# Split weights and inputs for gated-linear units 1 to 7, and v normalised by ACT, in a one-core encoder step

## The chip, the cores and the metric

The kernel runs on one core of a Trainium2 chip. The metric is the device time of one execution in microseconds (us). The engines of the core are named as in the profile: PE (matrix products), ACT (activations and copies), DVE (vector work), POOL (GpSimd), SP (issues most of the DMAs).

## What is computed

One step of a one-layer encoder on 512 prompt tokens and 32 sample tokens (T = 544 in all, D = 1024 features). The part that the change touches:

```python
z = h @ w_in + b_in                       # h: normalised, modulated input, 544 x 1024
a = glu(z[..., 0:2048])                   # first half * sigmoid(second half)
a = silu(layer_norm(depthwise_causal_conv(concat(history, a), conv_w, conv_b), ln_g, ln_b))
y_a = a @ w_a
u, v = gelu(z[..., 2048:3072]), gelu(z[..., 3072:4096])
v = layer_norm(v, v_ln_g, v_ln_b)         # v of the 32 sample rows is an output
y_b = (u * (tril(w_s) mixed over 128 positions of v + b_s)) @ w_b
merged = sigmoid(gates_a) * y_a + sigmoid(gates_b) * y_b
x = x + g1 * (merged @ w_o)
```

After it comes a mixture of 32 experts (top group, then top 2 of 8 in it) and a final norm. All inputs and outputs are float32.

## The kernel before, in words

Features lie on the partitions and tokens along the row, so that a product of 128 output features is `PS[128, 544]`, made in two halves of 272 columns. The mixer runs in stages, and each engine's order is written out by hand with semaphores.

- **GLU units 0 to 7** (`product`, L552). Unit n makes features 128n to 128n+127 of both halves of `a`, so two products, in plain float32 from `WP` (weights) and `hT` (input). ACT drains each unit (L989, L990, the last one the sigmoid; semaphore `act_drained`). SP may load unit n+2 into unit n's buffer when unit n is done (`w_used`).
- **v** (L656): nine groups in float32, drained by ACT through a gelu (L1020) into `v`, tokens on the partitions.
- **u units 0 to 3** (`product_split`, L619). Here a float32 factor is split in a high part (rounded to fp32r by an ACT copy: `wH` L1002, `gH` L998) and the rest (`wL`, `gL`, a DVE or POOL subtraction), and the product is the sum of three fp32r products, high by high, high by low and low by high. DVE makes the `wL` of the u units (`low_u`, L1277), each of them two instructions, one for each product; ACT makes the `wH` (`high_of`).
- **Gate units** 0 to 15 (`gate(j)`), two to each load, also in three products. POOL makes their `wL` (`low_gate`, L1699), two instructions for each pair of gates.
- **The mixing** (`mix(h)`, L683) needs `v` normalised (`v_norm`); a mean over features by PE (`over_features`, L690) waits for the sum of the convolved tiles (`conv_sum`).

DVE is the engine with the long job here: the depthwise convolution, 31 taps for each of 8 tiles of 574 columns, a pair of tiles at a time (i = 0, 2, 4, 6), two `scalar_tensor_tensor` for each tap (L1295). A pair begins when ACT has drained both of its units (`act_drained`). `low_u(0)` stands after pair 4, `low_u(1)` to `low_u(3)` after taps 9, 17 and 25 of pair 6. Then `add_tiles` sums the eight tiles (L1308, signals `conv_sum`), and then DVE takes the statistics of v (L1320), scales and shifts it (L1330 to L1332, `v_norm`) and subtracts the mean from the tiles (L1336, `centred`).

POOL's queue after the constants is `low_gate` 0 to 2, a store of the sample rows of v, `low_gate` 3 to 5, eight squares (L1713) and `low_gate` 6 to 15.

## Time and profile before

| | us |
|---|---|
| median of 3 runs (lowest, highest) | 937.46 (935.69, 938.75) |
| the profiled execution, its own time | 940.93 |
| its span, first to last instruction | 939.1 |
| PE busy | 837.4 (89%) |
| DVE busy | 504.8 (54%) |
| ACT busy | 191.3 (20%) |
| POOL busy | 156.5 (17%) |

The profiled execution is 3.5 us above the median. Its mean granted clock of PE is 0.949 of full speed. The page of the profile has one line for each group of instructions; a start is counted from the first instruction of the span. An instruction's duration may overlap the next one's on the same engine, so that the interval from start to start is the cost in a stream.

### The profile page before, as it was taken

The numbers are of one execution on the slowest core, as the hardware profiler recorded it, in microseconds if no ns is written. First come the engines' busy times: TensorE is split into PE (matmuls) and PEld (weight loads), VectorE is DVE, ScalarE is ACT, GpSimd is POOL, SyncE is SP. The second block draws the span as 40 slices with busy tenths as digits, with TensorE's granted clock in tenths as the row PEclk, the third lists the DMA queues.
The fourth block names the chain that finished last, engine by engine and source line by source line (L and its number), as shares of the span: only waits on it lengthen the run. The fifth ranks groups of instructions, "written<-read, shape, count | busy, mean of one in ns | idle before, by whom it ended". The sixth has DMA issues, their size and how long they took to land. (4 is left out here: it accounts for less than half of the span.)

```text
span 939.1 us, 12130 instructions
## 1 busy us (share of the span) xinstructions
PE 837.4 (89%) x4994; PEld 610.1 (65%) x4994; DVE 504.8 (54%) x754; ACT 191.3 (20%) x286; POOL 156.5 (17%) x152
## 2 busy tenths in 40 slices
PE   2899999999999999899999999628999988797776
PEld 1588887345999999798777544625666655454432
DVE  1427999999999735703755344661333331312236
ACT  4211121101225213821200022101111111111003
POOL 1000000000033345342322000011222221211110
PEclk9899999999999999999999999558999989989899
DMA  9932232211223313459899580614999999999926
GB/s 320 304 95 79 56 89 90 90 45 45 79 62 96 96 46 90 123 193 309 300 329 331 205 350 24 277 61 171 414 406 416 414 417 378 391 388 411 381 76 249
DMA packets 112600, 204.16 MB, mean 217 GB/s; under 512 B 9484, under 2 KB 68212, under 8 KB 104350
## 3 DMA queue, kind: packets, MB, share of 16 engines
q1 hardware_dynamic: 94192, 159.36, 47.8%
q10 hardware_dynamic: 12830, 34.93, 9.6%
q0 software_dynamic: 5520, 9.06, 2.6%
q8 instruction: 41, 0.67, 0.3%
q14 instruction: 17, 0.14, 0.0%
HBM read 199.49 MB, written 14.84 MB: 228 GB/s over the span
## 5 line engine op out<-in xcount | busy, mean ns | idle before, releaser
L862 PE MATMUL PS<-arena 128*64 128x256 f32 (+1 forms) x1056 | 148.6, 411 | 31.6 <-issue 26.5
L1295 DVE SCALAR_TENSOR_TENSOR arena<-arena,VT 128x574 f32<-128x574 f32 x240 | 175.2, 817 | 0.0
L862 PEld LDWEIGHTS PS<-arena 128*64 128x64 f32 (+1 forms) x1056 | 107.3, 157 | 68.1 <-issue 41.9
L1699 POOL TENSOR_TENSOR wL<-arena,wH 128x1024 fp32r<-128x1024 f32 x32 | 82.6, 2604 | 373.1 <-ACT wH L1002 373.1
L552 PE MATMUL PS<-arena 128*128 128x272 f32 x512 | 120.6, 399 | 1.6 <-DVE arena L1257 1.6
L552 PEld LDWEIGHTS PS<-arena 128*128 128x128 f32 x512 | 99.2, 194 | 22.6 <-issue 1.6
L1595 DVE TENSOR_TENSOR arena<-PS,arena 128x256 f32<-128x256 f32 x19 | 8.1, 425 | 141.5 <-ACT arena L1129 141.5
L619 PE MATMUL PS<-gH,wH 128*128 128x272 f32 x384 | 80.2, 290 | 1.9 <-DVE wL L1277 1.2
L619 PE MATMUL PS<-gH,wL 128*128 128x272 f32 x384 | 79.8, 289 | 0.0
L619 PE MATMUL PS<-gL,wH 128*128 128x272 f32 x384 | 79.7, 289 | 0.0
L882 PE MATMUL PS<-arena 128*64 128x512 f32 (+1 forms) x264 | 69.1, 597 | 1.4 <-DVE arena L1599 1.4
L1002 ACT ACTIVATE wH<-arena 128x1024 fp32r<-128x1024 f32 x40 | 40.2, 1052 | 122.8 <-DMA arena<-w_in 52.2
L1743 POOL DMA_INDIRECT pairs<-arena,sidx x19 | 30.4, 1600 | 193.4 <-DVE arena L1611 193.4
L619 PEld LDWEIGHTS PS<-gH,wH 128*128 128x128 f32 x384 | 59.9, 188 | 3.3 <-ACT arena L1020 1.5
L619 PEld LDWEIGHTS PS<-gH,wL 128*128 128x128 f32 x384 | 60.5, 188 | 0.0
L619 PEld LDWEIGHTS PS<-gL,wH 128*128 128x128 f32 x384 | 60.1, 188 | 0.0
L619 PE MATMUL PS<-yH,wH 128*128 128x272 f32 x256 | 54.7, 295 | 4.5 <-issue 4.5
L756 PE MATMUL PS<-arena 128*128 128x512 f32 x128 | 55.7, 593 | 0.7 <-DMA arena<-w_o 0.7
L656 PE MATMUL PS<-arena 128*128 128x512 f32 x128 | 56.2, 592 | 0.0
L619 PE MATMUL PS<-yH,wL 128*128 128x272 f32 x256 | 53.5, 290 | 0.0
L1129 ACT ACTIVATE arena<-PS 128x256 f32<-128x256 f32 x19 | 7.3, 384 | 210.2 <-PE PS L862 210.2
L619 PEld LDWEIGHTS PS<-yH,wH 128*128 128x128 f32 x256 | 40.4, 191 | 14.8 <-issue 11.4
(276 smaller groups left out, 978.4 us busy)
## 6 DMA issues: line engine op xcount, KB each, us to landing
arena<-w_gate SPq DMA_DIRECT2D x32, 1024.0 KB, 11.2
arena<-w_up SPq DMA_DIRECT2D x32, 1024.0 KB, 16.7
arena<-w_down ACTq DMA_DIRECT2D x28, 1024.0 KB, 15.2
arena<-w_ada SPq DMA_DIRECT2D x12, 2048.0 KB, 10.4
arena<-w_in SPq DMA_DIRECT2D x40, 512.0 KB, 5.2
arena<-w_ada_f SPq DMA_DIRECT2D x4, 2048.0 KB, 8.9
arena<-x_prompt SPq DMA_DIRECT2D x8, 512.0 KB, 8.2
arena<-w_in SPq DMA_DIRECT2D x4, 1024.0 KB, 6.4
```

Of the source, the lines that this page charges most:

```text
L552: last = pe.matmul(PS[:, bank + h, 0:H], tile_w[:, k, :], act[:, k, h * H:(h + 1) * H], start=(k == 0), stop=(k == KT - 1))
L619: last = pe.matmul(PS[:, bank + h, 0:H], w[:, k, :], part[:, k, h * H:(h + 1) * H], start=(k == 0 and n == 0), stop=(k == KT - 1 and n == 2))
L656: last = pe.matmul(PS[:, bank, :], hT[:, k, t * P:(t + 1) * P], W[hf][:, k, :], start=False, stop=(k == KT - 1))
L756: last = pe.matmul(PS[:, (2 * t + hf) % 8, :], mT[:, k, t * P:(t + 1) * P], W[hf][:, k, :], start=(k == 0), stop=(k == KT - 1))
L862: last = pe.matmul(PS[h * rows:(h + 1) * rows, 2, n * DE:(n + 1) * DE], hG[:, b, k * SLOTS + h * rows:k * SLOTS + (h + 1) * rows], buf[r / ...
L882: last = pe.matmul(PS[h * rows:(h + 1) * rows, 4 + 2 * b + hf, :], heT[:, k, h * rows:(h + 1) * rows], WD[r // 2][r % 2][:, k, hf * 512:(h ...
L1002: act.activation(wH2[n % 2][:, m], WP[n % 2][:, m], ACT.Copy).then_inc(gw_high, 1)
L1129: act.activation(sil, PS[:, 2, 0:DE], ACT.Silu).then_inc(sil_ready, 1)
L1295: dve.scalar_tensor_tensor(out=total, in0=src, scalar=tap, in1=total, op0=ALU.mult, op1=ALU.add).then_inc(conv_step, 1)
L1595: dve.tensor_tensor(he, PS[:, 2, DE:2 * DE], sil, ALU.mult).then_inc(he_ready, 1)
L1699: pool.tensor_tensor(wL2[q % 2][:, m], WP[q % 2][:, m], wH2[q % 2][:, m], ALU.subtract).then_inc(gw_split, 1)
L1743: pool.indirect_dma_start(out=pairs, out_offset=bass.IndirectOffsetOnAxis(ap=sidx[b][:, 0:1], axis=0), in_=Y[:, b, :], in_offset=None, bou ...
```

## The change

The rest of this section names lines of the kernel before. Unit 0 stays as it was. Units 1 to 7 of the GLU are made by `product_split`: ACT copies their high parts (`high_a`), DVE subtracts (`low_a`), all of `gH` is copied before unit 0's drain and all of `gL` subtracted before the first pair of the convolution. The `low_a` of units 3 to 7 stand inside pair 0 of the convolution, the `low_u` inside pairs 4 and 6, after other taps than before. Two new products on PE sum the rows of the mixing matrix (`rowsum_ps`); DVE folds `v_ln_b` times these sums into `bsb`, and multiplies by `v_ln_g` where it drains the mixing.

v is no longer normalised by DVE. The gelus of ACT write their sums, DVE makes the mean after tap 28 of pair 4, ACT squares and sums (five instructions) and takes the root, DVE makes scale and offset after tap 4 of pair 6, and ACT applies them (five instructions) after it has drained the first u unit. POOL then makes the 32 output rows of v with weight and bias (two instructions) ahead of `low_gate(0)`. `over_features` of the mean stands after `gate(3)`, before it stood after `gate(2)`. Of `b_in`, `v_ln_g` and `v_ln_b` only 1, 32 and 32 rows are loaded instead of 128 each, and 16 rows more go through the start's transposes.

```diff
+            for q in range(2):
+                last = pe.matmul(PS[:, 4 + q, :], meanm[:, :], wsT[:, 4 * q:4 * q + 4, :].rearrange("p h t -> p (h t)"), start=True, stop=True)
+            last.then_inc(rowsum_ps, 1)
+
+            def product_split(bank, w_high, w_low, act_high, act_low, split=None, split_of=None):
...
+                if n == 1:
+                    pe.wait_ge(rowsum_used, 1)
                 for m in range(2):
-                    last = product(4 * b + 2 * m, WP[b][:, m], hT, first=(n == 0))
+                    if n == 0:
+                        last = product(2 * m, WP[0][:, m], hT, first=True)
+                        continue
+                    pe.wait_ge(aw_split, 2 * n + m - 1)
+                    last = product_split(4 * b + 2 * m, wH2[b][:, m], wL2[b][:, m], gH, gL, 0 if (n, m) == (1, 0) else None, g_split)
...
             histories(FULL - HIST)
             gate(2)
+            gate(3)
             pe.wait_ge(conv_sum, 1)
             pe.wait_ge(hist_copied, 2)
             over_features(6, rstdc)
-            gate(3)
             gate(4)
             gate(5)
...
+            def high_a(n):
+                full(act, U_A + n)
+                for m in range(2):
+                    act.activation(wH2[n % 2][:, m], WP[n % 2][:, m], ACT.Copy).then_inc(aw_high, 1)
+
+            high_a(1)
+            act.wait_ge(h_odd, KT)
+            act.wait_ge(h_even, KT)
+            for j in range(KT):
+                act.activation(gH[:, j, :], hT[:, j, :], ACT.Copy).then_inc(g_high, 1)
             for n in range(KT):
                 b = 4 * (n % 2)
...
-                if n == 2:
-                    act.wait_ge(h_even, KT)
-                    act.wait_ge(h_odd, KT)
-                    act.wait_ge(bias_split, 3)
-                if n in (2, 3, 4, 5):
-                    for j in (2 * n - 4, 2 * n - 3):
-                        act.activation(gH[:, j, :], hT[:, j, :], ACT.Copy).then_inc(g_high, 1)
+                if n + 2 < KT:
+                    high_a(n + 2)
...
+                    total = {} if t == 4 else {"accum_out": vsum[:, t, hf:hf + 1]}
+                    act.activation(v[0:WIDTH[t], t, hf * 512:(hf + 1) * 512], src, ACT.Gelu_apprx_tanh, **total).then_inc(v_gelu, 1)
+                if g == 2:
+                    act.wait_ge(v_gelu, 4)
+                    act.activation(mg[0:NSAMPLE, :], v[0:NSAMPLE, 4, :], ACT.Copy, accum_out=vsum[0:NSAMPLE, 4, 0:1]).then_inc(v_sample, 1)
                 if g == 6:
                     high_of(U_U)
             high_of(U_U + 1)
+            act.wait_ge(v_mean, 1)
+            for t in range(TT):
+                w = WIDTH[t]
+                if t:
+                    act.wait_ge(v_sq, t)
+                act.activation(mg[0:w, :], v[0:w, t, :], ACT.Square, bias=mv[0:w, 0, t:t + 1], accum_out=vvar[0:w, t:t + 1]).then_inc(v_sq, 1)
+            act.wait_ge(v_sq, TT)
+            act.activation(vsd[:, 0:TT], vvar[:, 0:TT], ACT.Sqrt, bias=eps[:, :], scale=1.0 / D).then_inc(v_sd, 1)
...
+                if n == 0:
+                    act.wait_ge(v_scale, 1)
+                    for t in range(TT):
+                        vt = v[0:WIDTH[t], t, :]
+                        act.activation(vt, vt, ACT.Identity, scale=vsd[0:WIDTH[t], t:t + 1], bias=mv[0:WIDTH[t], 1, t:t + 1]).then_inc(v_norm, 1)
...
+            def low_a(n):
+                for m in range(2):
+                    dve.wait_ge(aw_high, 2 * n + m - 1)
+                    dve.tensor_tensor(wL2[n % 2][:, m], WP[n % 2][:, m], wH2[n % 2][:, m], ALU.subtract).then_inc(aw_split, 1)
+
+            then(dve.tensor_scalar(VT[:, COL_VB:COL_VB + KT], VT[:, COL_VB:COL_VB + KT], float(D), None, ALU.mult))
+            low_a(1)
+            for j in range(KT):
+                dve.wait_ge(g_high, j + 1)
+                dve.tensor_tensor(gL[:, j, :], hT[:, j, :], gH[:, j, :], ALU.subtract).then_inc(g_split, 1)
+
             dve.wait_ge(bc_in, 64)
+            dve.wait_ge(rowsum_ps, 1)
+            for h in range(KT):
+                soon(dve.scalar_tensor_tensor(out=bsb[:, h, :], in0=PS[:, 4 + h // 4, (h % 4) * P:(h % 4 + 1) * P], scalar=VT[:, COL_VB + h:COL_VB + h + 1],
+                                              in1=bsb[:, h, :], op0=ALU.mult, op1=ALU.add))
             then(dve.memset(b3, 0.0))
-            rest, piece = bvb[0:1, :], mod1[0:1, 0:D]
+            dve.sem_inc(rowsum_used)
+            rest, piece = bvb[0:1, :], mg[0:1, :]
...
+            low_a(2)
+            LOW_A = {(0, 3): 3, (0, 9): 4, (0, 16): 5, (0, 23): 6, (0, 29): 7}
+            LOW_U = {(4, 14): 0, (4, 27): 1, (6, 3): 2, (6, 10): 3}
...
-                    if i == 6 and k in (9, 17, 25):
-                        low_u((k - 1) // 8)
-                if i == 2:
-                    dve.wait_ge(g_high, KT)
-                    for j in range(KT):
-                        dve.tensor_tensor(gL[:, j, :], hT[:, j, :], gH[:, j, :], ALU.subtract).then_inc(g_split, 1)
-                if i == 4:
-                    low_u(0)
+                    if (i, k) in LOW_A:
+                        low_a(LOW_A[i, k])
+                    if (i, k) in LOW_U:
+                        low_u(LOW_U[i, k])
+                    if (i, k) == (4, 28):
+                        dve.wait_ge(v_gelu, 10)
+                        dve.wait_ge(v_sample, 1)
+                        then(dve.tensor_tensor(mv[:, 1, :], vsum[:, :, 0], vsum[:, :, 1], ALU.add))
+                        dve.tensor_scalar(mv[:, 0, :], mv[:, 1, :], -1.0 / D, None, ALU.mult).then_inc(v_mean, 1)
+                    if (i, k) == (6, 4):
+                        dve.wait_ge(v_sd, 1)
+                        then(dve.reciprocal(vsd[:, 0:TT], vsd[:, 0:TT]))
+                        dve.tensor_tensor(mv[:, 1, :], mv[:, 0, :], vsd[:, 0:TT], ALU.mult).then_inc(v_scale, 1)
...
-            dve.wait_ge(bc_in, 64)
-            for t in range(TT):
-                w = WIDTH[t]
-                dve.wait_ge(v_gelu, 7 + t if t < 4 else 4)
-                for hf in range(2):
-                    then(dve.bn_stats(bn[0:w, hf, :], v[0:w, t, hf * 512:(hf + 1) * 512]))
-                last = dve.bn_aggr(mv[0:w, t, :], bn[0:w, :, :].rearrange("p a b -> p (a b)"))
-                if t < TT - 1:
-                    then(last)
-            last.then_inc(v_var, 1)
-            dve.wait_ge(v_sd, 1)
-            then(dve.reciprocal(vsd[:, 0:TT], vsd[:, 0:TT]))
-            for t in range(TT):
-                w = WIDTH[t]
-                vt = v[0:w, t, :]
-                then(dve.tensor_scalar(vt, vt, mv[0:w, t, 0:1], vsd[0:w, t:t + 1], ALU.subtract, ALU.mult))
-                then(dve.tensor_tensor(vt, vt, vgb[0:w, :], ALU.mult))
-                dve.tensor_tensor(vt, vt, vbb[0:w, :], ALU.add).then_inc(v_norm, 1)
-
...
-                                  PS[:, 4 + 2 * b, :].rearrange("p (c t) -> p c t", t=P),
-                                  bsb[:, h:h + 1, :].to_broadcast([P, 4, P]), ALU.add).then_inc(mix_added, 1)
-                dve.tensor_tensor(tmp[:, b, NPROMPT:T], PS[:, 5 + 2 * b, 0:NSAMPLE], bsb[:, h, 0:NSAMPLE], ALU.add).then_inc(dve_drained, 1)
+                gain = VT[:, COL_VG + h:COL_VG + h + 1]
+                dve.scalar_tensor_tensor(out=tmp[:, b, 0:NPROMPT].rearrange("p (c t) -> p c t", t=P),
+                                         in0=PS[:, 4 + 2 * b, :].rearrange("p (c t) -> p c t", t=P), scalar=gain,
+                                         in1=bsb[:, h:h + 1, :].to_broadcast([P, 4, P]), op0=ALU.mult, op1=ALU.add).then_inc(mix_added, 1)
+                dve.scalar_tensor_tensor(out=tmp[:, b, NPROMPT:T], in0=PS[:, 5 + 2 * b, 0:NSAMPLE], scalar=gain,
+                                         in1=bsb[:, h, 0:NSAMPLE], op0=ALU.mult, op1=ALU.add).then_inc(dve_drained, 1)
...
+            pool.wait_ge(bc_in, 64)
+            pool.wait_ge(v_norm, TT)
+            rows = vgb[0:NSAMPLE, :]
+            pool.tensor_tensor(rows, v[0:NSAMPLE, 4, :], rows, ALU.mult).then_inc(v_gained, 1)
+            pool.wait_ge(v_gained, 1)
+            pool.tensor_tensor(rows, rows, vbb[0:NSAMPLE, :], ALU.add).then_inc(v_shifted, 1)
             low_gate(0)
-            low_gate(1)
-            low_gate(2)
-            pool.wait_ge(v_norm, TT)
-            pool.dma_start(v_out, v[0:NSAMPLE, 4, :]).then_inc(v_stored, 16)
-            low_gate(3)
-            low_gate(4)
-            low_gate(5)
+            pool.wait_ge(v_shifted, 1)
+            pool.dma_start(v_out, rows).then_inc(v_stored, 16)
+            for q in range(1, 6):
+                low_gate(q)
             pool.wait_ge(mix_ps, KT)
```

The first place is POOL's queue between the constants and the experts, in the kernel before. Line 1699 is `low_gate`, two rows for each of its calls, and line 1713 the squares.

```order
L1692 AFFINE_SELECT arena<-arena 128x128 x8
L1699 TENSOR_TENSOR wL<-arena,wH 128x1024 x6
L1705 DMA v_rows<-arena 32x1024
L1699 TENSOR_TENSOR wL<-arena,wH 128x1024 x6
L1713 TENSOR_TENSOR arena<-arena 128x574 x8
```

The same place in the changed kernel, where line 1742 is `low_gate` and lines 1747 and 1749 make the output rows of v:

```order
L1735 AFFINE_SELECT arena<-arena 128x128 x8
L1747 TENSOR_TENSOR arena<-arena 32x1024
L1749 TENSOR_TENSOR arena<-arena 32x1024
L1742 TENSOR_TENSOR wL<-arena,wH 128x1024 x2
L1752 DMA v_rows<-arena 32x1024
L1742 TENSOR_TENSOR wL<-arena,wH 128x1024 x10
L1758 TENSOR_TENSOR arena<-arena 128x574 x8
```

Two instructions that wait for the normalised v now stand ahead of the first `low_gate`.

The second place is DVE's last pair of the convolution before. Line 1295 is a tap of one tile, line 1277 `low_u`, line 1308 the sum of the tiles.

```order
L1292 TENSOR_SCALAR arena<-arena,VT 128x574 x2
L1295 SCALAR_TENSOR_TENSOR arena<-arena,VT 128x574 x18
L1277 TENSOR_TENSOR wL<-arena,wH 128x1024 x2
L1295 SCALAR_TENSOR_TENSOR arena<-arena,VT 128x574 x16
L1277 TENSOR_TENSOR wL<-arena,wH 128x1024 x2
L1295 SCALAR_TENSOR_TENSOR arena<-arena,VT 128x574 x16
L1277 TENSOR_TENSOR wL<-arena,wH 128x1024 x2
L1295 SCALAR_TENSOR_TENSOR arena<-arena,VT 128x574 x10
L1308 TENSOR_TENSOR rstdc<-arena 128x574
```

The same pair in the changed kernel (line 1348 is a tap, 1327 `low_u`, 1360 and 1361 the scale and offset of v, 1366 the sum):

```order
L1345 TENSOR_SCALAR arena<-arena,VT 128x574 x2
L1348 SCALAR_TENSOR_TENSOR arena<-arena,VT 128x574 x6
L1327 TENSOR_TENSOR wL<-arena,wH 128x1024 x2
L1348 SCALAR_TENSOR_TENSOR arena<-arena,VT 128x574 x2
L1360 RECIPROCAL vsd<-vsd 128x5
L1361 TENSOR_TENSOR mv<-mv,vsd 128x5
L1348 SCALAR_TENSOR_TENSOR arena<-arena,VT 128x574 x12
L1327 TENSOR_TENSOR wL<-arena,wH 128x1024 x2
L1348 SCALAR_TENSOR_TENSOR arena<-arena,VT 128x574 x40
L1366 TENSOR_TENSOR rstdc<-arena 128x574
```

The last `low_u` moved from ten taps ahead of the end of the pair to forty ahead of it.

## Rows read from the trace of the kernel before

**Rows 1.** Busy time of each engine in stretches of the span, with clock.

```profile
core 0: us, PE busy (x) PEld busy (x) DVE busy (x) ACT busy (x) POOL busy (x), PEclk, DMA share, GB/s
42.00:60.00 18.00, 17.21 (x62) 13.85 (x63) 8.96 (x16) 4.04 (x8) 0.00 (x0) 0.81 0.39 127
...
280.00:350.00 70.00, 69.67 (x543) 67.85 (x542) 50.34 (x69) 23.72 (x28) 27.12 (x13) 1.00 0.30 81
...
392.00:400.00 8.00, 3.50 (x18) 3.39 (x17) 3.58 (x6) 7.80 (x13) 0.00 (x0) 0.81 0.87 270
...
650.00:939.00 289.00, 249.69 (x1470) 152.60 (x1466) 89.45 (x110) 44.08 (x69) 53.66 (x69) 0.94 0.91 363
```

**Rows 2.** Timeline of PE: start, duration, instruction, count [idle before it].

```profile
42.79 120.57 PE L552 MATMUL PS<-arena 128*128 128x272 f32 x512 [1.57 <-DVE arena L1257]
...
229.90 0.52 PE L619 MATMUL PS<-gH,wH 128*128 128x272 f32 x2 [0.69 <-ACT arena L1020]
...
299.67 1.13 PE L690 MATMUL PS<-rstdc,meanm 128*128 128x287 f32 x4
...
318.78 1.05 PE L683 MATMUL PS<-wsT,arena 128*128 128x128 f32 x8
```

**Rows 3.** Timeline of ACT: sums with a read-out, table, drains of units.

```profile
12.87 1.06 ACT L952 ACTIVATE tmp<-arena 128x1024 f32<-128x1024 f32 x1
...
14.11 1.05 ACT L952 ACTIVATE tmp<-arena 32x1024 f32<-32x1024 f32 x1
...
15.28 1.28 ACT L954 ACT_TABLE_LOAD   x1
...
75.40 1.02 ACT L989 ACTIVATE arena<-PS,VT 128x272 f32<-128x272 f32 x3 [11.54 <-PE PS L552]
...
90.07 1.02 ACT L989 ACTIVATE arena<-PS,VT 128x272 f32<-128x272 f32 x3 [13.04 <-PE PS L552]
...
242.29 1.32 ACT L1033 ACTIVATE arena<-PS,VT 128x544 f32<-128x544 f32 x2 [4.27 <-PE PS L619]
248.16 2.01 ACT L1002 ACTIVATE wH<-arena 128x1024 fp32r<-128x1024 f32 x2 [4.55 <-DMA arena<-w_in]
254.40 1.32 ACT L1033 ACTIVATE arena<-PS,VT 128x544 f32<-128x544 f32 x2 [4.22 <-PE PS L619]
...
280.00 1.32 ACT L1033 ACTIVATE arena<-PS,VT 128x544 f32<-128x544 f32 x2 [5.68 <-PE PS L619]
```

**Rows 4.** Timeline of DVE: pair 0, the split of the inputs, a `low_u`.

```profile
77.06 1.50 DVE L1284 TENSOR_TENSOR arena<-arena 128x512 f32<-128x512 f32 x4 [19.70 <-ACT arena L990]
...
79.58 43.72 DVE L1295 SCALAR_TENSOR_TENSOR arena<-arena,VT 128x574 f32<-128x574 f32 x60
...
169.35 5.17 DVE L1301 TENSOR_TENSOR gL<-arena,gH 128x544 fp32r<-128x544 f32 x8
...
238.45 2.36 DVE L1277 TENSOR_TENSOR wL<-arena,wH 128x1024 fp32r<-128x1024 f32 x2
```

**Rows 5.** Timelines of POOL and DVE at the end of the convolution.

```profile
273.45 4.71 POOL L1699 TENSOR_TENSOR wL<-arena,wH 128x1024 fp32r<-128x1024 f32 x1 [248.12 <-ACT wH L1002]
...
272.88 3.02 DVE L1295 SCALAR_TENSOR_TENSOR arena<-arena,VT 128x574 f32<-128x574 f32 x4
275.94 2.84 DVE L1308 TENSOR_TENSOR rstdc<-arena 128x574 f32<-128x574 f32 x1
```

**Rows 6.** Timelines of POOL and DVE where both subtract and multiply.

```profile
385.79 2.97 POOL L1699 TENSOR_TENSOR wL<-arena,wH 128x1024 fp32r<-128x1024 f32 x1 [6.63 <-ACT wH L1002]
...
385.76 0.76 DVE L1365 TENSOR_TENSOR arena<-arena,rstdc 128x574 f32<-128x574 f32 x1
...
386.43 2.94 DVE L1365 TENSOR_TENSOR arena<-arena,rstdc 128x574 f32<-128x574 f32 x1
```

**Rows 7.** A POOL copy during a DVE instruction of the convolution's kind.

```profile
650.27 0.97 POOL L1739 COPY sidx<-pairI 128x1 uint32<-128x1 uint32 x1
...
649.91 1.29 DVE L1603 SCALAR_TENSOR_TENSOR tmp<-arena,wsel,tmp 128x1024 f32<-128x1024 f32 x1 [0.64 <-ACT tmp L1135]
```

46 lines of the change are left out of this document (23 added, 23 removed).

## The prediction, made before the changed kernel ran

> **What bounds the kernel now.** I read the table of stretches first, to see which engine is full and at what clock. From 280 to 350 us PE is busy for 69.67 of 70 us at clock 1.00, while DVE is busy for 50.34 and POOL for 27.12 [rows 1]. The late stretch, 650 to 939, is one of weight loads, with the DMA engines 0.91 busy; each load there waits for a buffer that the stage before has freed, so a delay or a gain of the mixer passes on whole. Then I read PE's timeline. The GLU stage is one block of 120.57 us from 42.79, the first u unit begins at 229.90, the mean over features stands at 299.67 and the first mixing at 318.78 [rows 2]. So in this kernel PE sets the end of the mixer. The third view, the timelines of DVE and POOL, asks whether PE stays the bound once it is faster. DVE runs its convolution without a break from 77.06 [rows 4] to the first sum at 275.94 [rows 5], 198.9 us. PE asks POOL for the first `low_gate` only when the u units are through, at 280.00 [rows 3]. Those two jobs hardly meet in the kernel before.
>
> **PE's own gain.** Two drains of float32 units lie 90.07 - 75.40 = 14.67 us apart, two of units in three products 254.40 - 242.29 = 12.11 us [rows 3]. Seven units save 7 x 2.56 = 17.9 us. Unit 0 before ended at 75.40 - 14.67 = 60.7. Two row sums of 512 columns now stand ahead of it, four records of float32. The rate of the float32 units (64 records of 272 columns in 14.67 us, so 0.43 us for 512) makes them 1.7 us at the full clock and 3.5 at half. That stretch has clock 0.81 over 18 us [rows 1], so it lost 3.4 us at half speed; PE now works without a pause from before unit 0, and its clock may rise sooner (unit 0 ends at 59.7) or as late as before (61.6). Unit 1 also needs both splits, the folding into `bsb` and a memset on DVE, some 11 us of ACT's and DVE's time after ACT's loads are issued, which is the same range. I take 60.5. Unit 7 then ends at 60.5 + 84.8 = 145.3. The v stage and its waits took 229.90 - 163.36 = 66.5, and the read-outs of the gelus add 0.2 at the last one, as two squares with a read-out are 14.11 - 12.87 = 1.24 us apart though one lasts 1.06 [rows 3]. The first u unit can start at 212.0, 17.9 us earlier than before.
>
> Does DVE keep up in the GLU stage? The drained unit's load, ACT copy and DVE subtraction need 248.16 - 242.29 = 5.9, then 1.0, then 1.2 us, in all 8.1 of the 12.1 that PE gives [rows 3, 4]. The `low_a` lie 6 or 7 taps apart, and a tap of two tiles costs 43.72 / 30 = 1.457, so one round is at most 10.2 + 2.4 = 12.6 us; starting with 2.3 us of slack they never make PE wait. I cost this at nothing.
>
> **DVE's job.** It begins 1.7 us after unit 1, as before (77.06 against 75.40), at 60.5 + 12.1 + 1.7 = 74.3. Against the 198.9 us: the split of the inputs goes out of it, -5.2; five `low_a` come in at 2.36, +11.8 [rows 4]; four instructions of five columns, +0.8. The u splits only move. The chain for v adds a wait. DVE makes the mean at 74.3 + (46.1 + 11.8) + 46.1 + 2.6 + 40.8 + 4.7 + 0.5 = 226.9 (pairs 0 and 2, the start of pair 4, 28 taps, two `low_u`); behind it ACT needs 5 x 1.24 for the squares, 1.28 + 0.3 for table and root, 1.28 for the next table, 1.32 for the drain of the first u unit and 1.0 for the next copy, and it is at 238.3. PE, ready for its third u unit at 236.2, starts it at 239.6, and DVE itself waits 1.3 us at that `low_u`. Without POOL the convolution thus ends at 74.3 + 198.9 - 5.2 + 11.8 + 0.8 + 1.3 = 281.9, 6 us later than before, although PE comes 14 us sooner. The statistics and scaling of v, which lay behind the sum of tiles, are gone from DVE, but PE was full from 280 to 350 [rows 1] and hardly waited for them, so that this is worth nothing by itself.
>
> **POOL beside the convolution.** This decides. PE now wants `low_gate(0)` at about 265, with 20 us of taps still to come; before it wanted it at 280, after them. The one row that shows a POOL subtraction issued inside the taps took 4.71 us. Four taps ran from 272.88 to 275.9, at their usual distance; three of them began after POOL's issue at 273.45, and then DVE's first sum, at 275.94, took 2.84 in place of the 0.76 of this size [rows 6], until POOL was done at 278.16 [rows 5]. A subtraction alone is 2.35 us (in [rows 6] POOL has the port from 386.41, when DVE's first instruction ends, to 388.76), so POOL began at 275.8, with the end of the last tap. A short POOL copy issued inside an instruction of the same kind ended with it, at 651.2 [rows 7]. So a tap keeps POOL out, and in a stream of taps POOL didn't get in at three boundaries out of three. In the likeliest case POOL's `low_gate(0)` therefore waits for the end of the convolution. The two output rows of v get in around the last `low_u`, where DVE's instructions are plain ones of two inputs, and cost 2 x 2.35: the convolution ends at 286.6. POOL's first subtraction is done at 289.0, and PE's gates begin there and not at 279.9, +9.1. PE has then stood for over 20 us. After a pause of 4.5 us the stretch from 392 to 400 had clock 0.81, which is 1.5 us lost; the start lost 3.4 [rows 1]. I take 2.4 between these. Behind that PE is the bound again: `conv_sum` comes at 286.6 + 7 sums of 0.79 + 4 POOL instructions = 301.5, and PE reaches the mean at 315. The sum is +9.1 + 2.4 = +11.5 us.
>
> The profiled execution has 939.1 of span and 940.93 of time, so it would become 952.4; on the median of the runs, 937.46, it is 949.0.
>
> The smaller edits cost nothing: the multiplication in the mixing's drain has one input in PSUM and hides in DVE's waits for the mixings; the two start loads and the smaller broadcasts lie beside PE's wait for weights; the later `over_features` only takes up a wait for `conv_sum`.
>
> **Rivals.** (a) POOL gets in at each boundary. Where DVE multiplies plainly, POOL, issued at 385.79, took 2.97, so it got in at the first boundary, and DVE's second instruction took 2.94 in place of 0.76 [rows 6]. That speaks for it; the taps of [rows 5] against. Then eight POOL instructions (two rows, six of `low_gate`) each push the taps by 2.2: the convolution ends at 281.9 + 17.6 = 299.5, the sum of tiles (5.5) with two more POOL instructions at 309.4. PE, early at its gates, waits for `conv_sum` and comes to the first mixing 1.1 + 12.1 later, at 322.6 against 318.78, +3.8, and 2.4 of clock make +6.2: 943.7. The Trainium skill, SBUF — State Buffer, section "SBUF: two separate sides", says that the shared port pair is an exclusive lock, that a DVE instruction with two SBUF inputs and a GpSimd one that reads SBUF compete for it, and that whichever starts first has it for the whole instruction. By that page POOL, which asks before the next tap, is this rival; the trace agrees on the lock [rows 6, 7] and not on who gets it [rows 5].
>
> (b) The other side: POOL doesn't disturb and is not disturbed, the long row in [rows 5] being only the first instruction of its kind on POOL. Then the `low_gate` come when called, the sum is done at 287.4, the u units end at 265, four gates and two histories at 291.3, and the first mixing begins at 304.5, -14.3: 923.2. It decides by the number of POOL instructions that fall ahead of the sum of tiles: with seven the sum comes at 302.8 and the first mixing at 316.0, and with 2.4 of clock the time is that of before; with none it is this. For it: PE's gain is real. Against it: [rows 6, 7].
>
> (c) Between: POOL gets in for the first `low_gate` but rarely after, and PE and DVE wait less for each other. Six POOL instructions ahead of the sum of tiles put it at 300.6 and the first mixing at 313.8, with the clock 934.9; nine put them at 307.2 and 320.4, with the clock 941.5.
>
> **How the numbers follow.** Chances: 0.50 for the forecast, 0.24 for (a), 0.13 for (b), 0.13 for (c), of which 0.08 lies within 0.3% (2.8 us, about what a measurement can tell from no change). So faster 0.13, same 0.08, slower 0.79. The low end of the range takes in (a), with its clock term at nothing too (941.3), and the upper part of (c), and leaves out (b) and the lower part of (c): 939. The high end is the forecast with the later unit 0 (+1.1), the larger clock term (+1.0) and POOL's rows behind the convolution too (+1.6), with a run's spread above it: 954.
>
> **What would show it.** In the changed profile: two GLU drains 12.1 us apart; the first u unit near 212; the last tap between 285 and 289; POOL's first subtraction of 128 x 1024 with a duration of over 20 us, and an idle time of PE of about 22 us that ends on it. If POOL's subtractions there last 2.4 to 3.2 us and taps of 3 us lie between the others, it is (a), and PE waits for `conv_sum`. If the taps keep their 0.73 and POOL its 2.35 at the same time, it is (b), and I am wrong about the port.

## The result, and the profile after

The changed kernel takes 942.31 us (median of 6 runs, 941.58 to 943.55) against 938.11 us for the kernel before on the same chip (6 runs, 935.69 to 943.84). The ratio is 1.0043, 95% interval 1.0024 to 1.0063: slower by 4 us, where 11.5 us slower was forecast. The profiled execution took 941.58 us, its span is 939.8 us and its mean granted clock 0.937. It lies 0.7 below its median, and that of before 2.8 above, so the two spans differ by 0.7 us only; I come back to this at the end of the section.

The stretches that answer to [rows 1], and two more, 270 to 290 and 290 to 310, which in the kernel before had PE busy throughout at clock 1.00:

```profile
42.00:60.00 18.00, 18.00 (x81) 14.63 (x80) 13.54 (x28) 10.95 (x20) 0.00 (x0) 0.95 0.32 58
270.00:290.00 20.00, 7.18 (x59) 6.78 (x56) 19.96 (x27) 7.58 (x9) 19.91 (x1) 0.74 0.24 65
290.00:310.00 20.00, 18.98 (x127) 18.77 (x128) 15.48 (x12) 1.43 (x2) 9.51 (x4) 0.84 0.16 45
392.00:400.00 8.00, 2.81 (x12) 2.85 (x13) 3.08 (x4) 7.94 (x12) 0.46 (x1) 0.72 0.92 282
```

PE has a new hole: from 270 to 290 it is busy for 7.18 us, while DVE is full and POOL shows one instruction that fills the stretch. Behind the hole the clock is 0.84 over 20 us; it is 0.50 from 291.02, where PE starts again, to 296.54, so 2.8 us of PE's work are lost there. PE's timeline, which answers to [rows 2]:

```profile
39.94 3.18 PE L616 MATMUL PS<-wsT,meanm 128*128 128x512 f32 x4
42.91 15.35 PE L556 MATMUL PS<-arena 128*128 128x272 f32 x64
58.08 0.48 PE L626 MATMUL PS<-gH,wH 128*128 128x272 f32 x2
...
209.69 0.52 PE L626 MATMUL PS<-gH,wH 128*128 128x272 f32 x2 [0.78 <-ACT arena L1040]
...
237.39 0.48 PE L626 MATMUL PS<-gH,wH 128*128 128x272 f32 x2 [3.24 <-DVE wL L1327]
...
291.02 0.82 PE L626 MATMUL PS<-gH,wH 128*128 128x272 f32 x2 [13.84 <-POOL wL L1742]
...
318.71 1.05 PE L695 MATMUL PS<-wsT,arena 128*128 128x128 f32 x8
```

The first u unit begins 20.2 us earlier than before. Two waits follow, and the first mixing begins at 318.71, where it began before (318.78). The whole gain of the three products is gone by then. The wait of 13.84 us stands ahead of gate 2: gates 0 and 1 and both history steps, 14.0 us of PE's work, were made before it, from 263.2 to 277.2. The drains of units on ACT, which answer to [rows 3], are 12.10 and 12.11 us apart, and the last u unit is drained at 263.38, 16.6 earlier than before:

```profile
70.46 1.02 ACT L1013 ACTIVATE arena<-PS,VT 128x272 f32<-128x272 f32 x3 [4.36 <-PE PS L626]
...
82.56 1.02 ACT L1013 ACTIVATE arena<-PS,VT 128x272 f32<-128x272 f32 x3 [3.65 <-PE PS L626]
...
94.67 1.02 ACT L1013 ACTIVATE arena<-PS,VT 128x272 f32<-128x272 f32 x3 [4.37 <-PE PS L626]
...
263.38 1.32 ACT L1064 ACTIVATE arena<-PS,VT 128x544 f32<-128x544 f32 x2 [3.80 <-PE PS L626]
```

POOL's timeline, which answers to [rows 5]:

```profile
246.10 7.26 POOL L1747 TENSOR_TENSOR arena<-arena 32x1024 f32<-32x1024 f32 x1 [220.37 <-ACT arena L1072]
253.44 2.78 POOL L1749 TENSOR_TENSOR arena<-arena 32x1024 f32<-32x1024 f32 x1
258.71 5.44 POOL L1742 TENSOR_TENSOR wL<-arena,wH 128x1024 fp32r<-128x1024 f32 x2 [2.49 <-ACT wH L1021]
264.10 0.75 POOL L1752 DMA_DIRECT2D v_rows<-arena  x1
270.09 29.42 POOL L1742 TENSOR_TENSOR wL<-arena,wH 128x1024 fp32r<-128x1024 f32 x4 [5.24 <-ACT wH L1021]
```

and DVE's, which answers to [rows 4, 5]:

```profile
72.11 1.50 DVE L1337 TENSOR_TENSOR arena<-arena 128x512 f32<-128x512 f32 x4 [4.57 <-ACT arena L1014]
...
248.77 2.35 DVE L1327 TENSOR_TENSOR wL<-arena,wH 128x1024 fp32r<-128x1024 f32 x2
251.04 37.72 DVE L1348 SCALAR_TENSOR_TENSOR arena<-arena,VT 128x574 f32<-128x574 f32 x40
288.80 2.78 DVE L1366 TENSOR_TENSOR rstdc<-arena 128x574 f32<-128x574 f32 x1
291.61 10.89 DVE L1366 TENSOR_TENSOR rstdc<-rstdc,arena 128x574 f32<-128x574 f32 x6
```

Here lies the answer. POOL was neither shut out throughout nor let in throughout. I call a tap pushed when it lasts about 2.95 us in place of 0.80, because POOL's instruction goes first. The first row of v waited for the end of the `low_u` at 251; the second row and both subtractions of `low_gate(0)` got in among the taps (5.44 us for two). The first subtraction of `low_gate(1)`, asked for at 270.09, was shut out until the last tap: of the row of four in 29.42 us it takes 20.88, and the others, which push DVE's first sums, 2.88 to 2.90 each. On DVE's side forty taps take 37.72 us. Where POOL does nothing among them they take 29.17 (below), so the four pushes (two rows of v, two subtractions) cost 2.14 us each.

**Where the 4 us are.** At the first mixing the two kernels are level. The drain of the first branch unit comes 1.3 us later, since PE's wait ahead of it is 5.55 instead of 4.50 us and the stretch from 392 to 400 has clock 0.72 instead of 0.81. In the router the distance is 1.05 us, by the same DVE instruction in both traces, first that of before, then that of after:

```profile
621.58 0.83 DVE L1554 TENSOR_TENSOR arena<-arena,iota 128x640 f32<-128x640 f32 x1
```

```profile
622.63 0.83 DVE L1595 TENSOR_TENSOR arena<-arena,iota 128x640 f32<-128x640 f32 x1
```

From there to the end it is 317.5 us before and 317.2 after. So the traces show 1.1 us of loss; the other 3 us of the medians lie in no stretch that these two executions show, and their cause stays open. On another chip one run of the changed kernel took 939.6 us against a median of 938.59 before.

### The profile page after: what moved, and what is told of

Read it like the earlier page. It is cut to its first block and busy times, and to the rows that moved or that the text cites. A ratio compares the mean times of both kernels' runs of the same rounds, so it can differ in the third digit from the quotient of the medians.

```text
span 939.8 us, 12626 instructions
## 1 busy us (share of the span) xinstructions
PE 824.3 (88%) x5222; PEld 611.1 (65%) x5222; DVE 511.5 (54%) x750; ACT 218.8 (23%) x324; POOL 184.2 (20%) x156
## 5 line engine op out<-in xcount | busy, mean ns | idle before, releaser
L1348 DVE SCALAR_TENSOR_TENSOR arena<-arena,VT 128x574 f32<-128x574 f32 x240 | 184.3, 841 | 0.0
L873 PEld LDWEIGHTS PS<-arena 128*64 128x64 f32 (+1 forms) x1056 | 105.5, 157 | 67.6 <-issue 42.0
L626 PE MATMUL PS<-gH,wH 128*128 128x272 f32 x608 | 127.8, 292 | 17.9 <-POOL wL L1742 13.8
L626 PE MATMUL PS<-gH,wL 128*128 128x272 f32 x608 | 128.0, 292 | 0.0
L626 PE MATMUL PS<-gL,wH 128*128 128x272 f32 x608 | 127.9, 292 | 0.0
L1742 POOL TENSOR_TENSOR wL<-arena,wH 128x1024 fp32r<-128x1024 f32 x32 | 100.1, 3150 | 136.1 <-ACT wH L1021 136.1
L626 PEld LDWEIGHTS PS<-gH,wH 128*128 128x128 f32 x608 | 96.2, 191 | 19.8 <-POOL wL L1742 14.1
L626 PEld LDWEIGHTS PS<-gH,wL 128*128 128x128 f32 x608 | 97.5, 192 | 0.0
L626 PEld LDWEIGHTS PS<-gL,wH 128*128 128x128 f32 x608 | 96.7, 191 | 0.0
L1747 POOL TENSOR_TENSOR arena<-arena 32x1024 f32<-32x1024 f32 x1 | 7.3, 7262 | 220.4 <-ACT arena L1072 220.4
L893 PEld LDWEIGHTS PS<-arena 128*64 128x64 f32 (+1 forms) x264 | 22.4, 145 | 34.1 <-issue 32.5
```

Of the source, the lines that this page charges most:

```text
L626: last = pe.matmul(PS[:, bank + h, 0:H], w[:, k, :], part[:, k, h * H:(h + 1) * H], start=(k == 0 and n == 0), stop=(k == KT - 1 and n == 2))
L873: last = pe.matmul(PS[h * rows:(h + 1) * rows, 2, n * DE:(n + 1) * DE], hG[:, b, k * SLOTS + h * rows:k * SLOTS + (h + 1) * rows], buf[r / ...
L893: last = pe.matmul(PS[h * rows:(h + 1) * rows, 4 + 2 * b + hf, :], heT[:, k, h * rows:(h + 1) * rows], WD[r // 2][r % 2][:, k, hf * 512:(h ...
L1348: dve.scalar_tensor_tensor(out=total, in0=src, scalar=tap, in1=total, op0=ALU.mult, op1=ALU.add).then_inc(conv_step, 1)
L1742: pool.tensor_tensor(wL2[q % 2][:, m], WP[q % 2][:, m], wH2[q % 2][:, m], ALU.subtract).then_inc(gw_split, 1)
```

## The experiments

The theory at the start: POOL waits for DVE at the port that the two share, and what is shut out, and when, sets the end. Its rivals: PE or ACT's order sets it, or the shutting out is chance. All times of before are from the same chip as the run beside them.

**The same kernel again.** No edit.

> The changed kernel once more, for its trace alone. If the way POOL is shut out of the taps of the convolution is fixed by the order of the instructions, the same rows come again: the first output row of v (L1747) lasts 7 us, the first subtraction of low_gate(1) about 20 us, and PE waits 13 to 14 us for it. If it is chance, other POOL instructions are the long ones, and the wait is anywhere between 0 and 20 us.

One run: 939.6 us (before 938.59). Everything from the first u unit on came some 1.6 us later, yet POOL's pattern is the same: 7.28, 2.78, then `low_gate(0)` in 2.40 and 2.90, then 20.36 us for the first subtraction of `low_gate(1)`; PE waits 13.9 us. The same instructions are shut out in both executions, so the order of work decides, not chance.

**Gates on DVE.** Everything stays but who makes the `wL` of gates 0 to 5, and that the rows of v stand behind `low_gate(4)`.

```diff
+            LOW_G = {(6, 17): 0, (6, 24): 1}
...
+                    if (i, k) in LOW_G:
+                        low_g(LOW_G[i, k])
...
             add_tiles(cv)
+            low_g(2)
...
-            low_gate(0)
-            for q in range(1, 6):
-                low_gate(q)
+            for q in range(3, 5):
+                low_gate(q)
```

> low_gate 0, 1 and 2 go from POOL to DVE (after taps 17 and 24 of the last pair, and after the sum of the tiles), and the two output rows of v go behind low_gate(4) on POOL. Theory 1 (the shared port: POOL's instructions are shut out of the taps, and push them when they get in): no POOL instruction meets a tap any more; DVE pays 4 x 1.15 inside the taps in place of 5 x 2.2, the last tap ends near 282, the sum near 288, PE reaches the mean over features near 290 and the first mixing near 303, so 12 to 15 us faster than the changed kernel: 927 to 931. Theory 2 (DVE's own work is too long, whoever subtracts): the sum of tiles comes at 295 or later and the gain is under 6 us: 936 or more.

925.18 us (924.12 to 925.72), ratio to before 0.9856 (0.9837 to 0.9875): 13.4 us faster than before. By the two ratios to before it is some 17 us faster than the change; against the one run of the change on this chip, 939.6, it is 14.4. PE's and DVE's timelines:

```profile
289.98 1.24 PE L702 MATMUL PS<-rstdc,meanm 128*128 128x287 f32 x4 [1.13 <-DVE rstdc L1374]
...
303.31 1.05 PE L695 MATMUL PS<-wsT,arena 128*128 128x128 f32 x8
```

```profile
263.12 10.26 DVE L1354 SCALAR_TENSOR_TENSOR arena<-arena,VT 128x574 f32<-128x574 f32 x14
...
284.41 0.76 DVE L1374 TENSOR_TENSOR rstdc<-arena 128x574 f32<-128x574 f32 x1
```

The two `low_g` beside these taps cost DVE 2.35 us each, 4.7 in all, where four pushes cost 8.6, the hole in PE is gone, and the first mixing begins 15.5 us earlier than before. So PE's gain was real, and POOL beside the taps took it. (This kernel changes two things; the rows of v moved by themselves are tried below, and that makes it slower.) The time is some 2 us better than the best I expected.

**ACT's order too.** The kernel above, with `low_g` after taps 14 and 22, and ACT's squares behind the drain of the first u unit.

```diff
-            act.wait_ge(v_mean, 1)
...
+                if n == 0:
+                    act.wait_ge(v_mean, 1)
...
                 high_of(U_U + n + 2)
```

> The changed kernel with low_gate 0 to 2 on DVE (0 and 1 after taps 14 and 22 of pair 6, 2 behind the sum of tiles), and with ACT's squares of v behind the drain of the first u unit instead of ahead of it, so that the copy for the third u unit isn't late. Theory 1 (POOL shut out cost the time, and the 3.2 us wait of PE for low_u is ACT's order): in the run with the gates on DVE alone PE still waited 3.2 us for DVE's wL and had a piece at half clock behind it; this wait falls under 1 us, and the time is 921 to 924 us, ratio to before 0.982 to 0.985. Theory 2 (DVE's sum of tiles is the bound then, and PE only waits there for what it gained): the wait before the mean over features grows from 1.1 us by what PE gained, first mixing at 302 to 303.5 us, time 924 to 926.

925.53 us (922.56 to 928.57), ratio 0.9866 (0.9842 to 0.989). PE's waits in the u units fell to 0.99 and 1.21 us and it reached the mean over features earlier, but the sum was not there:

```profile
288.60 1.24 PE L702 MATMUL PS<-rstdc,meanm 128*128 128x287 f32 x4 [1.96 <-DVE rstdc L1375]
...
303.46 1.05 PE L695 MATMUL PS<-wsT,arena 128*128 128x128 f32 x8
```

The mean starts 1.4 us earlier than in the kernel above, since the sum is done earlier (288.54 against 289.92), and the clock takes that back: it is 0.91 from 290 to 310, and 1.00 in the kernel above. Theory 2 has the first mixing and the time right and theory 1 has not: PE's 3.2 us wait for `low_u` was worth nothing here, in part because DVE's sum is the bound and in part by the clock.

**Pauses.** The changed kernel; from tap 12 of pair 6, each second tap waits until the one before it has ended.

```diff
-                            dve.wait_ge(conv_step, i * TAPS + (2 * (k - 1) + b + 1))
+                            dve.wait_ge(conv_step, i * TAPS + (2 * k if i == 6 and k > 11 and b == 0 else 2 * (k - 1) + b + 1))
```

> From tap 12 of the last pair each pair of taps waits until the tap just before it has ended, so that DVE stands still for about 0.1 us every 1.5 us; nothing else is changed. Theory 1 (POOL gets in wherever DVE pauses): the first subtraction of low_gate(1) lasts under 5 us in place of 20.9, PE waits not for POOL but for the sum of the tiles, which comes 2 us later than in the changed kernel for the pauses and no earlier, since the POOL instructions now push taps in place of sums: the mean over features near 304, the time 939 to 943. If PE's wait for POOL were all that costs, the time would be near 930. Theory 3 (POOL is kept out by something else than the seamless stream of taps): the 20 us row stays, and the time is 943 to 946.

945.76 us (942.45 to 947.58), ratio 1.0073 (1.0048 to 1.0098). POOL, DVE and PE:

```profile
271.17 5.83 POOL L1742 TENSOR_TENSOR wL<-arena,wH 128x1024 fp32r<-128x1024 f32 x2 [6.38 <-ACT wH L1021]
283.61 5.44 POOL L1742 TENSOR_TENSOR wL<-arena,wH 128x1024 fp32r<-128x1024 f32 x2 [6.61 <-ACT wH L1021]
296.74 5.15 POOL L1742 TENSOR_TENSOR wL<-arena,wH 128x1024 fp32r<-128x1024 f32 x2 [7.69 <-ACT wH L1021]
```

```profile
251.61 52.47 DVE L1348 SCALAR_TENSOR_TENSOR arena<-arena,VT 128x574 f32<-128x574 f32 x40
```

```profile
309.68 2.28 PE L702 MATMUL PS<-rstdc,meanm 128*128 128x287 f32 x4 [19.85 <-DVE rstdc L1366]
```

A pause of 0.1 us is enough: from tap 12 on every POOL instruction gets in, the 20.88 us are gone, and PE has its gates in time. But ten POOL instructions now fall among the taps (the second row of v and four pairs of subtractions, the first row behind the `low_u`), forty taps take 52.47 us, and PE waits 19.85 us for the sum instead. The sum is done at 309.62 and the first mixing begins at 325.01, before at 318.78. Letting POOL in costs about as much as shutting out `low_gate(0)` does (325.71 and a ratio of 1.0072, under "The rows of v last"). The time lies 3 us above what I expected and within the 943 to 946 of theory 3, but the trace, with the 20 us row gone, speaks for theory 1; the later convolution also caught `low_gate(3)`, two more pushes that I had not counted.

**The GLU half alone.** Units 1 to 7 in three products, the `low_u` and the mean over features placed as in the change; v is normalised by DVE as before and POOL makes no rows.

```diff
-                    last = product(4 * b + 2 * m, WP[b][:, m], hT, first=(n == 0))
+                    pe.wait_ge(aw_split, 2 * n + m - 1)
+                    last = product_split(4 * b + 2 * m, wH2[b][:, m], wL2[b][:, m], gH, gL, 0 if (n, m) == (1, 0) else None, g_split)
```

> The GLU half of the change alone: units 1 to 7 in three products, with the low_u and the mean over features placed as in the changed kernel; v is normalised by DVE behind the sum of tiles as before. Theory 1: the taps end at 282 to 288, the sum by 297, and 28 to 32 us of statistics and scaling follow, so that v is ready near 325 to 330 in place of 315, and PE waits there: 945 to 952. If DVE's queue did not matter, this half alone would give PE's 17 us: near 922.

950.45 us (947.66 to 952.17), ratio 1.0129 (1.0103 to 1.0155), +11.9 us.

```profile
255.49 32.92 POOL L1719 TENSOR_TENSOR wL<-arena,wH 128x1024 fp32r<-128x1024 f32 x4 [230.44 <-ACT wH L1013]
```

```profile
248.47 29.17 DVE L1319 SCALAR_TENSOR_TENSOR arena<-arena,VT 128x574 f32<-128x574 f32 x40
```

```profile
279.98 0.79 PE L620 MATMUL PS<-gH,wH 128*128 128x272 f32 x2 [20.09 <-POOL wL L1719]
...
321.59 1.05 PE L688 MATMUL PS<-wsT,arena 128*128 128x128 f32 x8
...
326.31 1.96 PE L688 MATMUL PS<-wsT,arena 128*128 128x128 f32 x8 [3.34 <-DVE arena L1356]
```

This is the forecast's mechanism: `low_gate(0)` is shut out from 255.5 to the last tap, 24.35 us for one subtraction. PE stands 20.09 us, and another 3.34 for the centred tiles, since DVE's work on v is on the path here. The time is in the range that I expected, but mostly for another reason: I had expected the wait for v alone and not the 20.09 us for POOL.

**The rows of v last.** The changed kernel with POOL's two rows behind `low_gate(4)`.

```diff
+            for q in range(0, 5):
+                low_gate(q)
             pool.wait_ge(bc_in, 64)
...
-            low_gate(0)
```

> The changed kernel with POOL's two output rows of v moved behind low_gate(4); DVE, ACT and PE unchanged. Theory 1 (whether POOL gets in is decided for each instruction by how it falls among the taps, and one that is issued in the middle of a seamless stream is mostly shut out to its end, as with the GLU half alone): low_gate(0), now issued near 253 to 255 us, lasts until the last tap, over 20 us, PE waits some 18 to 20 us for POOL before gate 0, last tap near 280 us (no pushes), time 942 to 950 us. Theory 2 (POOL gets in at about every second boundary by chance of its arrival): low_gate(0) lasts 2.4 to 3.2 us, low_gate(1) may be shut out, PE's wait stays near 14 us or less, time 938 to 943 us.

946.69 us (941.33 to 947.66), ratio 1.0072 (1.0049 to 1.0095).

```profile
259.76 33.40 POOL L1742 TENSOR_TENSOR wL<-arena,wH 128x1024 fp32r<-128x1024 f32 x4 [234.00 <-ACT wH L1021]
```

```profile
284.67 0.82 PE L626 MATMUL PS<-gH,wH 128*128 128x272 f32 x2 [20.00 <-POOL wL L1742]
...
325.71 1.05 PE L695 MATMUL PS<-wsT,arena 128*128 128x128 f32 x8
```

Two short instructions taken out of the way, and `low_gate(0)` is shut out for 24.86 us where it took 2.58. The taps go through unpushed, PE waits 20.00, and the first mixing comes 6.9 us later than before and 7.0 later than in the changed kernel, of which 1.9 were there at the first u unit (211.61 against 209.69). So the rows of v were what opened the door for `low_gate(0)` in the changed kernel.

**Bursts of POOL in the kernel before.** At four places of the convolution POOL multiplies three times on scratch memory; memsets of different sizes ahead of them shift where in a tap POOL asks. (Added work; ACT waits for it, so the times, 965.40 and 965.37 us, say nothing.)

```diff
+            for at, size in zip((20, 82, 144, 194), (0, 128, 256, 512)):
+                pool.wait_ge(conv_step, at)
+                if size:
+                    one(pool.memset(tmp2[:, 1, 0:size], 0.0))
+                both()
+                both()
+                one(pool.memset(tmp2[:, 1, 0:384], 0.0))
+                both()
```

> The kernel before with four bursts of POOL work on scratch memory during the convolution (each three multiplications of 128x1024, with a memset ahead of two of them), so the time is longer and not of interest. Theory 1 (a waiting POOL instruction is let in by a gap between DVE's instructions, such as a low_a, a low_u or the end of a pair, and by a boundary between two taps only sometimes): some of the 12 multiplications last 2.3 to 3.3 us, others over 5 us, up to the next instruction of DVE that is no tap; each one that gets in makes one tap 2.9 us long. Theory 2 (a tap always loses at its end to a waiting POOL instruction): all 12 last under 3.4 us. Theory 3 (the time within a tap at which POOL's instruction is issued decides): short and long ones separate by the distance from the last tap's start.

> The same bursts behind memsets of other sizes, so that the multiplications are issued at other distances from a tap's start. Theory 3: short and long ones separate at the same distance as in the other probe. Theory 1: both kinds occur at equal distances. Theory 2: all last under 3.4 us.

Two bursts of the first of them:

```profile
91.42 36.54 POOL L1710 TENSOR_TENSOR tmp<-arena 128x1024 f32<-128x1024 f32 x2 [65.96 <-DVE arena L1296]
...
128.72 2.50 POOL L1710 TENSOR_TENSOR tmp<-arena 128x1024 f32<-128x1024 f32 x1
...
143.86 40.96 POOL L1710 TENSOR_TENSOR tmp<-arena 128x1024 f32<-128x1024 f32 x2
```

In all eight bursts the first multiplication is shut out: in pairs 0, 2 and 4 through every tap that is left of the pair, in pair 6 until the next `low_u` has ended (34.0, 38.1, 35.2 and 12.5 us; 33.8, 38.6, 34.9 and 12.8 in the other kernel), while the second and third, asked for 0.1 and at most 0.8 us behind the end of POOL's last multiplication, are done in 2.85 us at most, the third among taps as well. The point within a tap plays no part: first ones were asked for at 0.07 to 0.69 us into one. A boundary of another kind isn't safe either: the 38.1 us went past the end of the taps and all eight subtractions of 128x544 from 173.92 on. The memsets, which read nothing, last 0.15 to 0.63 us and are never held up for the length of a tap. Theories 2 and 3 fall. Theory 1, that a gap of another kind lets POOL in, is right in part only, and does not say when a boundary between taps does.

**How long the door stays open.** One tap pauses, POOL asks k taps later, and a second pause follows 8 taps behind the call; nine times in each kernel.

```diff
+                            at = i * TAPS + 2 * k + b
+                            dve.wait_ge(conv_step, at if at in PAUSES else at - 1)
...
+            for n, at in enumerate((7, 27, 47, 72, 92, 112, 137, 157, 177)):
+                pool.wait_ge(conv_step, at)
+                pool.tensor_tensor(tmp2[:, 1, 0:1024], vgb[:, 0:1024], vbb[:, 0:1024], ALU.mult).then_inc(probed, 1)
```

> The kernel before, with nine POOL multiplications of 128x1024 on scratch memory in pairs 0, 2 and 4 of the convolution. Each is asked for k taps behind a tap that had to wait until the one before it had ended (a pause of about 0.1 us), k from 1 to 9 in this order, and another such pause follows 8 taps behind the call. Theory 1 (a POOL instruction is let in at a boundary of taps only if DVE's stream was broken a short while before, by a pause, by POOL itself or by another kind of instruction): those for k of 1 to 3 last 2.3 to 3 us, those for k of 7 to 9 last about 8 us, until the second pause lets them in; the border lies between 4 and 7 taps, since 2.5 us after a break it was let in and 5.4 us after it not. Theory 2 (chance): no order in k. Theory 3 (a pause itself is needed at the boundary at which POOL waits): all nine last until the second pause, about 8 us.

> The same with k in the order 9, 7, 6, 5, 8, 4, 3, 2, 1. Theory 1: the same border in k, now with the long ones first. Theory 2: no order. Theory 3: all last about 8 us.

POOL in the first, k = 1, 5, 6, 7, 9, and in the second, k = 9, 6, 5:

```profile
82.39 2.78 POOL L1707 TENSOR_TENSOR tmp<-arena 128x1024 f32<-128x1024 f32 x1 [57.49 <-DVE arena L1298]
...
154.63 2.79 POOL L1707 TENSOR_TENSOR tmp<-arena 128x1024 f32<-128x1024 f32 x1 [14.10 <-DVE arena L1298]
171.51 2.79 POOL L1707 TENSOR_TENSOR tmp<-arena 128x1024 f32<-128x1024 f32 x1 [14.09 <-DVE arena L1298]
198.18 7.88 POOL L1707 TENSOR_TENSOR tmp<-arena 128x1024 f32<-128x1024 f32 x1 [23.87 <-DVE arena L1298]
...
231.69 7.87 POOL L1707 TENSOR_TENSOR tmp<-arena 128x1024 f32<-128x1024 f32 x1 [8.88 <-DVE arena L1298]
```

```profile
87.23 7.87 POOL L1707 TENSOR_TENSOR tmp<-arena 128x1024 f32<-128x1024 f32 x1 [61.45 <-DVE arena L1298]
...
117.11 7.88 POOL L1707 TENSOR_TENSOR tmp<-arena 128x1024 f32<-128x1024 f32 x1 [7.43 <-DVE arena L1298]
137.10 2.79 POOL L1707 TENSOR_TENSOR tmp<-arena 128x1024 f32<-128x1024 f32 x1 [12.12 <-DVE arena L1298]
```

| k | 1 | 2 | 3 | 4 | 5 | 6 | 7 | 8 | 9 |
|---|---|---|---|---|---|---|---|---|---|
| first kernel, us | 2.78 | 2.79 | 2.80 | 2.79 | 2.79 | 2.79 | 7.88 | 7.88 | 7.87 |
| second kernel, us | 2.78 | 2.78 | 2.79 | 2.79 | 2.79 | 7.88 | 7.88 | 7.87 | 7.87 |

The order in k is complete in both. Up to 5 taps behind a pause (POOL asks 3.9 us behind the paused tap's start) it gets in at the next boundary, from 7 taps on (5.3 us) it doesn't, and at 6 (4.6 us) it did once and once not. Those shut out last 7.9 us: until the second pause, which lets them in. This rule fits every POOL instruction of the changed kernel that meets the taps: the first row was asked for 6.1 us behind DVE's last wait and shut out, the second row was asked for 0.1 us behind POOL's own last one, `low_gate(0)` 1.9 us behind the end of the tap that POOL had pushed (256.8), `low_gate(1)` 5.3 us behind the end of the last pushed one (264.8). It fits the others too. The subtraction of [rows 5] was asked for 4.9 us behind the first tap after the last `low_u` and shut out, `low_gate(0)` 7.0 us behind it with the GLU half alone and 6.5 us with the rows last; in the bursts of pair 6 it was 5.2 and 4.9 us, both shut out.

**The v half alone, twice.** All GLU units in float32; ACT normalises v, POOL makes the rows first. In the second kernel the mean and scale of v come later on DVE.

```diff
-                    if (i, k) == (4, 28):
+                    if (i, k) == (6, 1):
...
-                    if (i, k) == (6, 4):
+                    if (i, k) == (6, 8):
```

> The v half of the change alone (ACT normalises v, weight and bias folded, POOL makes the output rows ahead of low_gate(0)); all eight GLU units in float32 with the splits of the inputs and the low_u where they were before. Theory 1 (the whole gain and the whole loss come from the GLU half, and the rows of v only lengthen the convolution by what POOL takes): PE keeps its block to 163 us and its u units to 280; the rows get in at boundaries behind a low_u, 2 x 2.2 us onto the convolution, which ends near 280; low_gate(0) is done near 283 and PE waits about 3 us; time 937 to 942 us. Theory 2 (v's own chain costs): PE waits over 2 us ahead of the third u unit or the first mixing, time over 943 us. Theory 3 (v's half pays, because DVE's normalisation was on the path): time under 935 us.

> The v half alone again, with DVE's mean of v after tap 1 of pair 6 and the scale after tap 8, since with PE in float32 the last gelus of v come only at 229.5 us and DVE stood 12.2 us at the mean in the run before this one. Theory 1 (the v half by itself is neutral but for POOL's rows): DVE waits under 1.5 us for v in all; the rows cost it 2 x 2.2 us; the last tap ends at 280 to 284 us, PE waits 2 to 6 us for low_gate(0) or the third wL; time 938 to 943 us. Theory 2 (the chain through ACT, squares ahead of the drain and copy, costs PE more than that): PE waits over 6 us for wL in the u units, time 944 to 950 us.

957.41 us (ratio 1.0202, 1.0161 to 1.0242) and 952.32 us (1.0147, 1.0121 to 1.0173). I had expected about no change, and missed that the places of v's instructions in DVE's order are set for a PE that is 17.9 us ahead. In both runs theory 2 has the reason, and the second is 2 us above its range too. DVE in the first kernel stands at the mean:

```profile
229.48 0.16 DVE L1334 TENSOR_TENSOR mv<-vsum 128x5 f32<-128x5 f32 x1 [12.21 <-ACT arena L1032]
```

PE then waits 17.0 us in three waits for DVE's `wL` in the u units. With the places moved DVE still waits 3.09 and 5.52 us for v, since ACT's squares come no sooner, and PE 12.1. So v's half, in these two orders, is a loss of 14.6 us or more without the GLU's, and the GLU's half loses 11.9 us alone; together they lose 4. They can't be added up.

## Why the prediction was wrong

Direction right, size wrong: +11.5 us forecast, +4.2 measured, and 942.3 lies in the range of 939 to 954 by luck: the range reached that low for rival (a), which is not what happened. By its steps:

- *PE's own gain*: right. Drains 12.1 us apart, and the `low_a` made PE wait nowhere.
- *"I take 60.5"* for the end of unit 0: 58.1 measured, below even the range from 59.7. The row sums took 3.18 us, but unit 0 began at 42.91, before at 42.79, so they cost 0.1; and the clock in that stretch was 0.95 instead of 0.81. The first u unit came at 209.69, not 212.0. This term was 2.4 us too large.
- *v's chain*: right. PE waited 3.24 us at the third u unit (forecast: ready at 236.2, start at 239.6), DVE 1.83 (1.3).
- *"So a tap keeps POOL out, and in a stream of taps POOL didn't get in at three boundaries out of three."* This is the step that failed. It is true only of a POOL instruction that asks long after DVE's last break. The row it rested on [rows 5] was such a one. The forecast then let the two rows of v in and did not ask what they change for the instruction behind them. They let `low_gate(0)` in, PE made gates 0 and 1 from 263.2 on, and its wait moved to gate 2 and shrank from 20.0 us (rows last) to 13.84. The shutting out itself was real, but it struck `low_gate(1)`. The forecast's wait ends at 289.0, with 38.9 us of PE's work and 2.4 of clock up to the first mixing, so 330.3; measured, it ends at 291.0, with 38.9 - 14.0 of work and 2.8 of clock, so 318.7. That is the failed step in numbers: 14.0 us of PE's work were done ahead of the wait and not behind it. It accounts for the first mixing; of the 4.2 us that remain in the time, the traces show 1.1. Without that door, the forecast's mechanism gives what the kernel with the rows last showed, a first mixing 6.9 us late (1.9 of them from earlier work) and a ratio of 1.0072, so 6.8 us by the ratio and 8.3 by the medians, not 11.5.
- *Last tap at 286.6, in 285 to 289*: 288.76 measured, with four pushes and not two, from a start 2.2 us earlier.
- *"I take 2.4"* for the clock: 2.8 us behind the hole, near enough; another 1.7 behind PE's wait at 237 (clock 0.86 from 238 to 250) were not in the sum, and went into the wait that followed.
- *Rival (a)* was priced at 943.7, close to the result by its number only. Its mechanism, PE waiting for the sum, needs all POOL instructions let in, and is the kernel with pauses (19.85 us of waiting, 945.76). Its point held: both shutting POOL out and letting it in cost PE. The 2.35 us for a subtraction, here and in the forecast, rest on a start at 386.41; by [rows 6] DVE's first instruction ends at 386.52, which would give 2.24. Undisturbed subtractions in the trace after take 2.36 to 2.40 (327.98, 312.51), so the number was right and its derivation loose.
- *Rival (c)* said what POOL did: let in for the first `low_gate`, but rarely after. The forecast gave it 0.13. It had PE and DVE wait less for each other, and did not ask where PE stands when the second `low_gate` is the one shut out. Its two prices are 934.9 and 941.5, with the first mixing at 313.8 and 320.4 by the end of the sum of tiles; measured are 942.3 and 318.7, and what PE waited for was POOL, not the sum.
- *Rival (b)*, no contention, 923.2, is nearly what the gates on DVE gave, 925.2, although DVE then does 4.7 us more work ahead of the sum.

The Trainium skill, SBUF — State Buffer, section "SBUF: two separate sides", says that whichever of the two starts first has the port pair for its whole instruction while the other fully blocks. The trace agrees on the block (a pushed tap about 2.95 us, POOL 2.78 to 2.90). On who is first, the page speaks of one instruction; here one "whole instruction" of DVE was not the measure, since a waiting POOL instruction was passed by more than 40 taps in 34 us, and the measurement decides.

## What to carry to other kernels

In this kernel a vector stream of two-input instructions without a gap held up a waiting GpSimd instruction to the stream's end, 20 to 25 us, and a stream with breaks paid 2.1 us for each that got in. So look twice before work that another engine waits for is given to GpSimd while DVE runs such a stream; giving DVE the few subtractions itself was worth 14 to 17 us here. When a change makes one engine faster, look at what its earlier request now meets: here 17.9 us of PE's gain turned into a wait for a helper that used to be called behind the stream. Two halves of a change that share an order of instructions can't be priced apart: alone these two gave ratios of 1.0129 and 1.0147 at best, together 1.0043.

## What was not expected of the hardware

- A POOL instruction with two inputs in SBUF asked for 4.9 us or more behind the last break of a stream of DVE `scalar_tensor_tensor` (4.9 to 16 us in these runs) was shut out until the stream ended or broke, up to 38.6 us; asked for up to 3.9 us behind the break it got in at the next boundary. The border is at 6 taps (4.6 us), where both happened. Breaks were a pause of 0.1 us, POOL's own turn, or the passage from a `low_u` to a tap, at which the first row of v and two of the bursts got in. The passage from taps to the eight subtractions of 128x544 was no such break. Whether time or the number of instructions counts was not separated.
- A pause of 0.12 us per two taps let all eight in. Nineteen such pauses come to 2.3 us; the price is the 2.1 us of each push.
- PE's wait of 1.96 us ahead of the mean was followed by clock 0.91 from 290 to 310, one of 1.13 us at the same place by clock 1.00.
